# An fp32 mixer layer on one core: four square buffers, the norm's factors inside the sums, keys taken earlier, a third stage set, an earlier mixing product and a reordered tail

## What is computed

```python
h = rmsnorm(x, norm_g)
ua, va, ga, q, k, v, gb, xc, gc = split(h @ w_in)           # w_in: 2048 x 5120
ya = gelu(ua) * (masked_w_s @ layernorm(gelu(va)) + b_s)    # blocks of 128 tokens
yb = sliding_window_attention(q, k, v, sinks, rel_bias)     # 16 query heads, 4 key heads of 64
yc = pooled_means_minus_token(xc) @ w_pool * c_scale        # windows 2, 4, 8, 16
mix = concat(ya * silu(ga), yb * silu(gb), yc * silu(gc))
return rmsnorm(x + mix @ w_out, final_g)
```

## Time and profile before

| | |
|---|---|
| runs | 1254.3 us median of 3 (1252.33 to 1254.41) |
| profiled execution | 1256.24 us, span 1254.4 us, mean granted clock 0.986 |
| TensorE busy | 96% of the span, 6118 matmuls |
| VectorE, ScalarE, GpSimd busy | 69%, 41%, 5% |
| DMA | 357.12 MB, mean 285 GB/s |

### The profile page before, as it was taken

One profiled execution on the slowest core, in us unless ns is written; L12 is line 12 of the kernel. 1 busy time (PEld: TensorE's weight loads), 2 busy tenths in 40 slices (PEclk: granted clock), 3 DMA queues, 4 the chain that ended last, 5 costly groups with the idle time before them and its releaser, 6 DMA issues.

```text
span 1254.4 us, 16226 instructions
## 1 busy us (share of the span) xinstructions
PE 1201.8 (96%) x6118; PEld 983.6 (78%) x6118; DVE 868.5 (69%) x1131; ACT 508.9 (41%) x900; POOL 64.7 (5%) x70
## 2 busy tenths in 40 slices
PE   7996979999999999999999999999899899999996
PEld 6885858888888888888888877778777688888884
DVE  6656486564778676679775797987966556664566
ACT  7466672422454443354533343233341412323135
POOL 3420300000000000000000000000000000000000
PEclk9998989999999999999999999999899999999998
DMA  8996689857785456796657678578999779965778
GB/s 311 322 327 241 236 313 393 308 201 256 281 315 205 160 199 263 269 337 266 234 185 253 243 292 294 194 280 314 410 384 375 297 290 387 407 241 202 288 285 332
DMA packets 106926, 357.12 MB, mean 285 GB/s; under 512 B 11328, under 2 KB 14432, under 8 KB 95712
## 3 DMA queue, kind: packets, MB, share of 16 engines
q1 hardware_dynamic: 106848, 356.08, 76.9%
HBM read 284.47 MB, written 71.57 MB: 284 GB/s over the span
## 4 chain that ended last, share of the span: by engine, by line
PE 75%; DVE 10%; DMA 6%; ACT 4%; SPq 2%; issue 2%; POOL 1%; ACTq 0%; DVEq 0%; POOLq 0%
PE n_bank L1674 21%; PE n_bank L1676 21%; PE n_bank L1675 21%; PE e_bank L1839 2%; PE t_bank L1867 2%; DVE w_lo L1180 2%; PE t_bank L1674 1%; PE t_bank L1850 1%; PE t_bank L1675 1%; PE t_bank L1676 1%; DMA m_parts<-stage_b 1%; DMA s_ring<-x_parts 1%; DMA x<-x_t_dram 1%; DMA m_parts<-stage 1%; ACT stage L943 1%
## 5 line engine op out<-in xcount | busy, mean ns | idle before, releaser
L1674 PE MATMUL n_bank<-s_ring,w_hi 128*128 128x512 f32 x896 | 357.9, 399 | 4.5 <-DVE tg L1320 3.8
L1676 PE MATMUL n_bank<-s_ring,w_lo 128*128 128x512 f32 x896 | 349.9, 391 | 0.0
L1675 PE MATMUL n_bank<-s_ring,w_hi 128*128 128x512 f32 x896 | 349.7, 390 | 0.0
L882 ACT ACTIVATE w_hi<-w_b 128x1024 fp32r<-128x1024 f32 x168 | 168.5, 1050 | 441.0 <-PE n_bank L1676 403.3
L1180 DVE TENSOR_TENSOR w_lo<-w_b,w_hi 128x1024 fp32r<-128x1024 f32 x168 | 198.0, 1220 | 120.1 <-ACT w_hi L882 119.9
L1674 PEld LDWEIGHTS n_bank<-s_ring,w_hi 128*128 128x128 f32 x896 | 168.8, 188 | 45.5 <-DVE tg L1320 4.6
L1676 PEld LDWEIGHTS n_bank<-s_ring,w_lo 128*128 128x128 f32 x896 | 168.8, 188 | 35.9
L1675 PEld LDWEIGHTS n_bank<-s_ring,w_hi 128*128 128x128 f32 x896 | 168.8, 188 | 35.6 <-issue 1.9
L1674 PE MATMUL n_bank<-w_hi,s_ring 128*128 128x512 f32 x448 | 176.3, 393 | 6.6 <-DMA s_ring<-m_parts 5.4
L1675 PE MATMUL n_bank<-w_lo,s_ring 128*128 128x512 f32 x448 | 175.0, 391 | 0.0
L1676 PE MATMUL n_bank<-w_hi,s_ring 128*128 128x512 f32 x448 | 174.8, 390 | 0.0
(11 more groups left out here) (227 smaller groups left out, 1507.7 us busy)
## 6 DMA issues: line engine op xcount, KB each, us to landing
s_ring<-x_parts SPq DMA_DIRECT2D x224, 512.0 KB, 5.9
w_b<-w_b_dram SPq DMA_DIRECT2D x64, 1024.0 KB, 10.5
s_ring<-m_parts SPq DMA_DIRECT2D x112, 512.0 KB, 6.0
raw<-w_dram SPq DMA_DIRECT2D x14, 1024.0 KB, 8.1
m_parts<-stage SPq DMA_DIRECT2D x20, 512.0 KB, 8.5
x_parts<-stage SPq DMA_DIRECT2D x32, 256.0 KB, 3.0
x_parts<-op_hi SPq DMA_DIRECT2D x12, 512.0 KB, 8.6
x_parts<-op_lo SPq DMA_DIRECT2D x12, 512.0 KB, 9.0
```

Source lines behind the costliest of these rows:

```text
L882: sc.activation(w_hi[:, J % 2, part], w_source(J)[:, part], ACT.Copy).then_inc(hi_done, 1)
L1674: pe.matmul(psum_out, stat[0], mov[0], start=first, stop=False)
L1675: pe.matmul(psum_out, stat[0], mov[1], start=False, stop=False)
L1676: return pe.matmul(psum_out, stat[1], mov[0], start=False, stop=last)
```

## The change

1. **Squares.** `x_sq` has four buffers (slot k mod 4) at another address, and ScalarE waits for GpSimd only from the fifth square on. The second half's squares wait for the first half's keys.
2. **x jobs.** ScalarE scales only tile a22, then writes a21 scaled straight into the stage; the other factors go into VectorE's sums as scalars (`x_sums`, with `minus_g_sb` = -`norm_g`). The first two high parts wait for two sums, not four. Jobs 4 and 5 move from J = 10, 11 to J = 9, 10, and job 5 stands ahead of chunk 3.
3. **Keys.** `keys` becomes `take_keys`, ahead of the weights' low parts, and `keys_lo`, after them.
4. **Loads.** Chunks 2 and 3 are loaded at J = 7 and 9, late in SyncE's list of that group.
5. **Third stage set.** `stage_c` (pairs 4 and 5) lies over a quadrant that is free then; m, s and t jobs of steps 49 to 58 get new steps and pairs.
6. **Mixing.** `mixed_0` (now over another quadrant) is loaded at step 47, `mixed_1` at 49; `mixed_0 * gate` is done at step 49, its product with `a_out` at 52.
7. **Tail.** Row blocks 0 and 1 share one root; `y12`'s multiplication by `final_g` is done at step 80, `y22`'s goes into the scaling.

The diff, cut:

```diff
+SQUARES = 4
...
-JOBS = tuple((t, "x", r, (0, 1)) for r, t in enumerate((5, 6, 7, 8, 10, 11, 12, 13))) + (
+JOBS = tuple((t, "x", r, (0, 1)) for r, t in enumerate((5, 6, 7, 8, 9, 10, 12, 13))) + (
...
-    (s2(46), "m", 8, (1,)), (s2(48), "m", 9, (0,)), (s2(48), "m", 10, (1,)), (s2(50), "s", 4, (2, 3)),
-    (s2(50), "m", 11, (1,)), (s2(52), "t", 4, (2,)), (s2(52), "s", 5, (0, 1)), (s2(54), "t", 5, (0,)),
-    (s2(54), "m", 12, (3,)), (s2(54), "m", 13, (2,)), (s2(55), "m", 14, (1,)), (s2(56), "m", 15, (3,)),
-    (s2(57), "s", 6, (0, 1)), (s2(58), "t", 6, (2,)), (s2(58), "s", 7, (0, 1)), (s2(58), "t", 7, (3,)))
+    (s2(46), "m", 8, (1,)), (s2(48), "m", 9, (0,)), (s2(48), "m", 10, (1,)), (s2(49), "m", 11, (4,)),
+    (s2(50), "s", 4, (0, 5)), (s2(51), "t", 4, (1,)), (s2(53), "m", 12, (2,)), (s2(53), "m", 13, (3,)),
+    (s2(54), "s", 5, (0, 5)), (s2(55), "t", 5, (1,)), (s2(55), "m", 14, (4,)), (s2(55), "m", 15, (2,)),
+    (s2(56), "s", 6, (3, 5)), (s2(57), "t", 6, (0,)), (s2(57), "s", 7, (1, 4)), (s2(58), "t", 7, (2,)))
+STAGES = 6
...
-        x_sq = place("x_sq", [P, 2, HS], offset=at_bias)
+        x_sq = place("x_sq", [P, SQUARES, HS], offset=at_vp)
+        stage_c = place("stage_c", [P, 4, HS], F32R, offset=at_b[3])
+        stages = (stage[:, 0:2, :], stage[:, 2:4, :], stage_b[:, 0:2, :], stage_b[:, 2:4, :],
+                  stage_c[:, 0:2, :], stage_c[:, 2:4, :])
-        mixed_0 = place("mixed_0", [P, 4, HS], offset=at_a[0])
+        mixed_0 = place("mixed_0", [P, 4, HS], offset=at_a[1])
...
-                if n == STEPS * PAIR_A + 9:
-                    sp.wait_ge(c_done, 8)
+                if n == STEPS * PAIR_A + 5:
+                    sp.wait_ge(pool_in, 6)
                     sp.wait_ge(mixed_saved, 32)
                     sp.dma_start(mixed_0[:], mixed_dram[0]).then_inc(mixed_loaded[0], 16)
-                if n == STEPS * PAIR_A + 10:
+                if n == STEPS * PAIR_A + 7:
                     wait_stored(sp, "t", 3)
                     sp.dma_start(mixed_1[:], mixed_dram[1]).then_inc(mixed_loaded[1], 16)
                 if n == STEPS * PAIR_A + 13:
+                    sp.wait_ge(a_done, 1)
...
-                if J == 8:
-                    wait_stored(sp, "x", 1)
-                    load_x1(2)
-                if J == 10:
-                    wait_stored(sp, "x", 3)
-                    load_x1(3)
...
+                if J == 7:
+                    wait_stored(sp, "x", 1)
+                    load_x1(2)
+                if J == 9:
+                    wait_stored(sp, "x", 3)
+                    load_x1(3)
...
-                if k >= 3:
-
-                    sc.wait_ge(x_acc_done, (KT - 1) * half + k - 2)
+                if k > SQUARES:
+
+                    sc.wait_ge(x_acc_done, (KT - 1) * half + k - SQUARES)
                 elif half == 1:
 
                     sc.wait_ge(x_acc_done, KT - 1)
-                sc.activation(x_sq[:, k % 2, :], src, ACT.Square).then_inc(x_sq_done, 1)
+                    sc.wait_ge(k_lo_done, 2)
+                sc.activation(x_sq[:, k % SQUARES, :], src, ACT.Square).then_inc(x_sq_done, 1)
...
+                if 4 in pairs or 5 in pairs:
+                    wait_stored(sc, "s", 3)
                 if kind == "x":
                     sc.wait_ge(x_sq_done, KT + 4 * (i // 2) + 4)
                     sc.wait_ge(x_lo_done, KT + 4 * (i // 2) + 4)
-                    for n, tile in enumerate(x_job_tiles(i)):
-                        k = 2 * i + n % 2
-                        sc.activation(tile, tile, ACT.Copy, scale=norm_g_sb[:, k:k + 1]).then_inc(xs_scaled, 1)
                     a11, a12, a21, a22 = x_job_tiles(i)
+                    sc.activation(a22, a22, ACT.Copy, scale=norm_g_sb[:, 2 * i + 1:2 * i + 2]).then_inc(xs_scaled, 1)
+                    wait_stored(sc, kind, i, after=False, pairs=pairs)
+                    sc.wait_ge(sums_made, sums + 2)
+                    split_item(tiles[0][:, 0, :], a22)
+                    sc.activation(tiles[0][:, 1, :], a21, ACT.Copy, scale=norm_g_sb[:, 2 * i:2 * i + 1]
+                                  ).then_inc(s_hi_done, 1)
                     sc.wait_ge(sums_made, sums + 4)
-                    wait_stored(sc, kind, i, after=False, pairs=pairs)
-                    for n, lo in enumerate((a22, a21, a11, a12)):
-                        split_item(tiles[n // 2][:, n % 2, :], lo)
+                    split_item(tiles[1][:, 0, :], a11)
+                    split_item(tiles[1][:, 1, :], a12)
...
+                if J == X1_BUILT[3]:
+                    job("x", 5)
...
+            last_square(0)
+            last_square(1)
+            second_root(0, 2, 2)
+            for st in range(2):
+                second_scale(y21[PAIR_O], st, 2)
+                second_scale(y22[PAIR_O], st, 2)
+            last_square(2)
+            second_root(2, 1, 3)
+            second_scale(y21[PAIR_O], 2, 3)
+            last_square(3)
+            second_root(3, 1, 4)
+            second_scale(y22[PAIR_O], 2, 3)
+            second_scale(y21[PAIR_O], 3, 4)
+            second_scale(y22[PAIR_O], 3, 4)
...
+            def x_sums(i, n):
+
+                a11, a12, a21, a22 = x_job_tiles(i)
+                gain, minus = norm_g_sb[:, 2 * i:2 * i + 1], minus_g_sb[:, 2 * i:2 * i + 1]
+                ve.wait_ge(xs_scaled, i + 1)
+                ve.scalar_tensor_tensor(out=a22, in0=a21, scalar=gain, in1=a22, op0=ALU.mult, op1=ALU.add
+                                        ).then_inc(sums_made, 1)
+                ve.tensor_tensor(a21, a11, a21, ALU.subtract).then_inc(sums_made, 1)
+                ve.wait_ge(sums_made, n + 1)
+                ve.scalar_tensor_tensor(out=a11, in0=a11, scalar=minus, in1=a22, op0=ALU.mult, op1=ALU.add
+                                        ).then_inc(sums_made, 1)
+                ve.wait_ge(sums_made, n + 3)
+                ve.scalar_tensor_tensor(out=a12, in0=a12, scalar=norm_g_sb[:, 2 * i + 1:2 * i + 2], in1=a11,
+                                        op0=ALU.mult, op1=ALU.subtract).then_inc(sums_made, 1)
+                ve.wait_ge(sums_made, n + 4)
...
+                if g == G_VA:
+                    take_keys(half)
                 if J >= 2:
                     split_lo(J + 1)
                 if g == G_VA - 1:
                     row_norms(half)
                 if g == G_VA:
-                    keys(half)
+                    keys_lo(half)
...
-                if J == step(PAIR_A, 11):
+                if J == step(PAIR_A, 7):
                     ve.wait_ge(mixed_loaded[0], 16)
+                    ve.wait_ge(y_gated, 7)
+                    settle(ve.tensor_tensor(mixed_0[:], mixed_0[:], y11[PAIR_A][:], ALU.mult))
+                if J == step(PAIR_A, 10):
                     ve.wait_ge(y_gated, 8)
-                    settle(ve.tensor_tensor(a_out[0][:], a_out[0][:], mixed_0[:], ALU.mult))
-                    ve.tensor_tensor(a_out[0][:], a_out[0][:], y11[PAIR_A][:], ALU.mult).then_inc(a_done, 1)
+                    ve.tensor_tensor(a_out[0][:], a_out[0][:], mixed_0[:], ALU.mult).then_inc(a_done, 1)
...
-                                       step(PAIR_O + 1, 5), step(PAIR_O + 1, 13))):
+                                       step(PAIR_O + 1, 5), step(PAIR_O + 1, 10))):
...
+            add_chain(PAIRS - 1, Q_A22, (0, 1))
+            second_root(0, 2, 2)
+            second_norm(0, 2)
+            second_norm(1, 2)
+            add_chain(PAIRS - 1, Q_A22, (2,))
+            second_root(2, 1, 3)
+            add_chain(PAIRS - 1, Q_A22, (3,))
+            second_norm(2, 3)
+            second_root(3, 1, 4)
+            second_norm(3, 4)
```

96 lines of the change are left out of this document (47 added, 49 removed).

## The result

| | before | changed |
|---|---|---|
| time, median (lowest to highest) | 1253.32 us (1251.16 to 1254.41, 4 runs) | 1235.03 us (1233.32 to 1236.21, 4 runs) |
| profiled execution: time, span | 1256.24, 1254.4 us | 1233.32, 1231.5 us |
| ratio | | 0.9853, 95% interval 0.9832 to 0.9875 |

The change makes the kernel 18.3 us faster; the forecast was 1223.5 with a range of 1210 to 1241. So sign and range held, and the time came out 11.5 us above the forecast. What the traces must explain is therefore 22.9 us against the 30.8 of the sum.

What follows compares the result with a forecast made beforehand. TensorE, busy 1201.8 of 1254.4 us, was taken to bound the kernel, leaving its stalls to gain. Front -17.5, middle -13 and tail -0.3 sum to -30.8, carried to the median: 1223.5 us, range 1210 to 1241.

Steps and rivals of the forecast that it cites:

- the three stretches: Where TensorE stood: the front before step 0, the passage from pair A to pair O, and the end storing results.
- the stall of 4.3 us at group 11: Front, start of weight group 11: a new TensorE stall of about 4.3 us, as job 5 delays the last chunk.
- rival (c): Tail: the end follows the chain of engines, not the stores, and gives 2.9 us: 1220.9 us; chance 0.07.
- Rival (d): Middle: added stores and loads in SyncE's one queue delay `s_ring` loads, stalling ten steps: about 1287 us, slower; chance 0.05.
- Front: -17.5 us: Start to step 0: step 0 begins at 203 instead of 220.5; bounds -24 and -11.
- stores from 91.4: Front, x job 1: its stores leave from 91.4 instead of 101.38, so job 2 can go on at 99.2.
- 0.6 + 1.4 (two sums) + 1.2 + 0.1 + 1.2 = 4.5 us: Front, ScalarE's time for one x job: 4.5 us instead of 7.6, so 3.1 us less.
- 8.3 us to the last square sum: Front, from ScalarE taking up the last chunk to the end of its square sums: 8.3 us, before 8.8.
- Rival (a): Front and middle: waits come back elsewhere, front -11 (job 5 holds the chunk), middle -3 (DMA queue): 1240 us; chance 0.19.
- The middle: Step 50 to the end of step 61: -13 us of 19.3 us excess; bounds -19 and -3.
- 3.8 + 2.6 us: Middle, step 53: moving VectorE's two products removes TensorE's 3.8 us stall and 2.6 us of lost clock.
- 3 us for late loads of step 61: Middle's end: full DMA engines bring the loads of step 61 about 3 us late, with 2 us of clock behind.

Runs made afterwards that it cites:

- small adds: From the changed kernel, GpSimd adds only 16 of 512 columns in the second half, leaving its row factors wrong: 1228.90 us.
- the kernel with the last chunk first: From the changed kernel, job 5 goes back behind the last chunk of x on ScalarE and VectorE, still in weight group 10: 1226.71 us.
- held adds: Job 5 behind the last chunk, and GpSimd's adds of the first three chunks held until the x job's sums behind that chunk are made: 1227.81 us.
- the split waits: Job 5 behind the last chunk, x jobs waiting for each stage pair's stores separately, and an early one-column gelu for the table load: 1224.30 us.

## Why the prediction was right in sign and wrong in size

**Right.** TensorE's stalls were what could be had, and the three stretches were the right ones. The kernel got faster; no wait for `k_stage` or `tg` is left; the stall of 4.3 us at group 11 is there with 4.1, though both its ends came more than 5 us later than forecast (141.8 to 145.9 for 136.2 to 140.5), so its size is partly luck; the last store ends 12 us behind TensorE; the tail ends with the stores, and undoing its order changes nothing, so rival (c) falls; the output leaves at 380 GB/s again, and not at the 436 that the Trainium skill's page DMA: Bandwidth & Descriptors gives in its section Bandwidth as the fabric's rate. For transfers between HBM and SBUF, which these stores are, that section of the Trainium skill gives about 358 as the limit; rival (c) left this out, and the trace lies above it. Rival (d) falls as well: `s_ring` lands in 10.8 us, and its waits are 2.9 us in all.

**The term that failed is "Front: -17.5 us".** It came out at -11.2, and at -10.0 from the first weights of group 5 on (69.82 before, 68.59 in the changed kernel, 69.09 with small adds), which is what the times below are counted from. The step in it is "stores from 91.4", that is, when job 1 is done. Two things were wrong there.

First, "0.6 + 1.4 (two sums) + 1.2 + 0.1 + 1.2 = 4.5 us" took the sums at 0.7 us. Beside GpSimd they take 1.75. I had weighed the rule of the Trainium skill (page SBUF — State Buffer, section on its two separate sides) that the two engines exclude each other, and applied it to GpSimd's adds and the statistics alone, as a loss of 2.8 us that I then left out. The traces show a loss on both engines, as the rule would have it. VectorE loses 1.05 us for each sum that meets an add, seven times. GpSimd's adds went from 1411 to 1651 ns, 3.6 us over fifteen, and 2.0 of these fall on the last chunk's four (7.50 for 5.50). By that rule, taken for both engines, the forecast would have been nearer.

Second, the forecast let job 1 go ahead without a wait for job 0's stores. In the changed kernel that wait is hidden, since the slow sums are later still; with small adds it is 5.1 us. Job 1's first store was forecast 21.6 us after the first weights; it left after 24.9 with small adds and after 27.5 in the changed kernel. So of 5.9 us, counted in this order, 3.3 are this omission and 2.6 the slow sums.

Both put job 2's go-ahead at 34.7 us (forecast 29.4), and `va` at 5.1 us of stall, where 0 to 1 was forecast. The chunk is then 6.2 us late (75.4 for 69.2), and 1.6 us more came between it and step 0: the 7.8 us between the forecast's 133.2 and the 141.0 measured. These 1.6 are a third term: "8.3 us to the last square sum" came out at 10.7 (154.69 - 143.98), by GpSimd's slow adds, and the rest of that sum was 0.8 us too long, 0.6 of it by its own arithmetic (its terms from 139 on make 201.8, not 202.4). Rival (a) had -11 for the front, from a chunk that job 5 holds and that comes no earlier than 145.85. The place is right; the chunk came at 143.98, so that the size agrees is partly chance, and its middle (-3) did not come.

**The middle was right in its sum for a wrong reason.** -11.6 against -13. I gave 3.8 + 2.6 us to the moved products. With both products back at step 53 the middle takes 0.8 us longer, 0.5 more than the longest of the same code. What is worth something is where the transfers stand: the two loads of `mixed` ahead of the full stretch (5.6 us when undone together with the products, beyond these alone), and the third stage set with its table (9.7 us in the trace when undone, 6.5 by the medians). The three amounts make 16.1 us by the traces and some 12 by the medians, against the 11.6 won, so whether they overlap can't be told; undoing all of them at once was not run. I had estimated 3 us for late loads of step 61, with 2 us of clock behind them. The changed kernel has 2.9 us of `s_ring` waits, but in eight pieces of at most 0.8, and no clock is lost, so the likeness of the two numbers is chance.

**The parts of the change, by what undoing them showed.** Four square buffers: nothing. The keys ahead of the split: nothing. The tail's order: nothing. The products: under 1 us. The loads of `mixed`: some 6 us. The third set with its table: 6.5 us by the medians, 9.7 in the trace. Job 5 ahead of the last chunk: a loss of 6 to 8 us, which the change carries. The rest of the front (the jobs' earlier groups, the shorter job, the chunk's earlier load) was not undone piece by piece; by the front of the kernel with the last chunk first it is worth 17 us, which is, by chance, what was forecast for the whole.

## What to carry to other kernels

Where an engine is freed of one wait, follow it to the next on the same resource: here the jobs go through two stage pairs, so a quicker job meets the stores of the one before it. When an edit makes GpSimd and VectorE work in SBUF at the same time, price the operations of both at their slow duration, and add up each engine's path. Before crediting a moved instruction with a stall, ask what a TensorE delay costs when the DMA queue is the next bound: the queue may give back what the stall took, and the load that moved with the instruction may be the part that counts.

## What was not expected of the hardware

- A 128x512 operation of VectorE with operands in SBUF took 0.68 to 0.75 us alone and 1.73 to 1.84 us when it met an add of GpSimd of the same size (1.4 to 1.65 us on average). The loss per meeting is some 1.05 us, for `tensor_tensor` and `scalar_tensor_tensor` alike, and VectorE pays it wherever the adds are put: held adds made four low parts 5.80 instead of 2.74 us. GpSimd pays as well: four adds took 5.50 us in the kernel before and 7.50 in the changed one. With adds of 16 columns (384 ns on average) no operation of VectorE was slow.
- A stall of 2.5 us left TensorE's granted clock at 1.00, which is 2.4 GHz; stalls of 4.1 and 5.1 us were followed by 0.50, 1.2 GHz, for some microseconds. What the kept clock is worth was not isolated: with the split waits the stall fell by 2.6 us and the median by 2.4, while a wait of 1.6 us for the statistics, which comes and goes between traces, stood against it.
- The same front, in five kernels, took 140.7 to 142.6 us, and what lies ahead of it varied by 1.4 us. A single trace does not tell 1 us in this stretch.
